# Expert weights in pieces of 8 KB: a change of the row order in the expert matmuls of a two-layer decoder trunk

## What is computed

```
for l in range(DEPTH):
    mod = silu(c) @ w_ada[l] + b_ada[l]                   # six rows of 1024: sh1, sc1, gt1, sh2, sc2, gt2
    u = x * (1 + sc1) + sh1
    mix = mlstm_and_conv(u @ w_in[l]) @ w_out[l]
    x = layer_norm(ALPHA * x + (1 + gt1) * mix)
    u = x * (1 + sc2) + sh2
    comb = route(u @ w_grp[l], u @ w_router[l])           # two experts a token, with weights
    for e in range(16):                                   # w_gate, w_up: (1024, 512); w_down: (512, 1024)
        h = silu(u @ w_gate[l][e]) * (u @ w_up[l][e])
        y = y + (h * comb[:, e]) @ w_down[l][e]
    x = layer_norm(ALPHA * x + (1 + gt2) * y)
```

## Time and profile before

| what | value |
|---|---|
| runs | 959.11, 959.91, 959.81 us (median 959.81) |
| span of the profiled execution | 958.0 us |
| TensorE busy (PE) | 851.8 us, 89% |
| weight loads into TensorE (PEld) | 437.7 us |
| VectorE, ScalarE busy | 246.4 us, 137.5 us |
| from HBM | 297.57 MB, 312 GB/s over the span |
| chain that ended last, by engine | PE 69%, SyncE's queue 14%, DMA 6%, VectorE 4%, ScalarE's queue 3% |

### The profile page before, as it was taken

One profiled execution on the slowest core, in us unless ns is written; L12 is line 12 of the kernel. 1 busy time (PEld: TensorE's weight loads), 2 busy tenths in 40 slices (PEclk: granted clock), 3 DMA queues, 4 the chain that ended last, 5 costly groups with the idle time before them and its releaser, 6 DMA issues.

```text
span 958.0 us, 9822 instructions
## 1 busy us (share of the span) xinstructions
PE 851.8 (89%) x3985; PEld 437.7 (46%) x3989; DVE 246.4 (26%) x679; ACT 137.5 (14%) x260; POOL 12.5 (1%) x42
## 2 busy tenths in 40 slices
PE   4349999998999999999879999999899999999881
PEld 1238478444534444344226847844443344434330
DVE  0012236236311110111063213614630111101106
ACT  1021110102201110011032111010310111101111
POOL 2100000000000000000001000000000000000000
PEclk9769999998999999999997999999999999999996
DMA  9993424768999999999999943486999999999981
GB/s 320 370 370 105 174 90 175 280 247 313 335 386 386 386 386 387 387 387 387 386 386 391 343 157 106 158 305 228 366 337 387 386 386 387 387 387 387 387 317 44
DMA packets 152562, 299.11 MB, mean 312 GB/s; under 512 B 8912, under 2 KB 9040, under 8 KB 152528
## 3 DMA queue, kind: packets, MB, share of 16 engines
q1 hardware_dynamic: 144288, 291.58, 83.2%
q0 software_dynamic: 1888, 6.82, 1.8%
q10 hardware_dynamic: 6352, 0.23, 0.5%
HBM read 297.57 MB, written 1.05 MB: 312 GB/s over the span
## 4 chain that ended last, share of the span: by engine, by line
PE 69%; SPq 14%; DMA 6%; DVE 4%; ACTq 3%; ACT 2%; issue 2%; another core or an unknown queue 0%; DVEq 0%
PE bank L474 16%; PE bank L441 15%; SPq L279 11%; PE bank L500 8%; PE bank L452 6%; PE bank L622 6%; PE bank L461 5%; DMA ring<-in_w_ada_dram 4%; PE bank L511 3%; PE bank L393 2%; DMA ring<-in_w_down_dram 2%; ACTq L755 2%; SPq L303 2%; DVE qT L951 2%; PE bank L562 1%
## 5 line engine op out<-in xcount | busy, mean ns | idle before, releaser
L474 PE MATMUL bank<-ring,qT 128*64 128x512 f32 x1024 | 227.1, 595 | 6.3 <-DMA ring<-in_w_gate_dram 3.4
L474 PEld LDWEIGHTS bank<-ring,qT 128*64 128x64 f32 x1024 | 73.4, 137 | 155.1 <-issue 144.9
L441 PE MATMUL bank<-uT,ring 128*128 128x256 f32 x640 | 139.9, 380 | 0.0
L441 PEld LDWEIGHTS bank<-uT,ring 128*128 128x128 f32 x640 | 121.1, 190 | 18.8 <-issue 2.7
L500 PE MATMUL bank<-ring,hb 128*64 128x512 f32 x512 | 113.8, 596 | 3.7 <-DMA ring<-in_w_down_dram 2.7
L959 DVE TENSOR_TENSOR o_sig<-o_sig,bank 128x512 f32<-128x512 f32 x16 | 11.0, 688 | 265.9 <-PE bank L474 241.5
L500 PEld LDWEIGHTS bank<-ring,hb 128*64 128x64 f32 x512 | 35.6, 137 | 70.7 <-issue 69.2
L461 PEld LDWEIGHTS bank<-ccT,X 128*128 128x128 f32 x512 | 58.5, 192 | 12.3 <-issue 11.4
L393 PE MATMUL bank<-ring,cond 128*32 128x512 f32 x384 | 50.4, 658 | 14.7 <-DMA ring<-in_w_ada_dram 13.4
L461 PE MATMUL bank<-ccT,X 128*128 128x128 f32 x512 | 61.2, 278 | 0.0
L511 PE MATMUL bank<-kT,hb 128*128 128x512 f32 x128 | 59.2, 605 | 0.0
(11 more groups left out here) (198 smaller groups left out, 495.2 us busy)
## 6 DMA issues: line engine op xcount, KB each, us to landing
ring<-in_w_gate_dram SPq DMA_DIRECT2D x32, 2048.0 KB, 19.2
ring<-in_w_up_dram SPq DMA_DIRECT2D x32, 2048.0 KB, 19.6
ring<-in_w_down_dram SPq DMA_DIRECT2D x32, 2048.0 KB, 18.1
ring<-in_w_ada_dram SPq DMA_DIRECT2D x24, 2048.0 KB, 14.1
ring<-in_w_in_dram SPq DMA_DIRECT2D x14, 2048.0 KB, 23.5
ring<-in_w_out_dram SPq DMA_DIRECT2D x4, 2048.0 KB, 8.0
gate_row<-in_b_ada_dram POOLq DMA_DIRECT2D x4, 512.0 KB, 9.6
ln_g<-in_ln_g_dram POOLq DMA_DIRECT2D x4, 512.0 KB, 11.2
```

Of the source, the lines that this page charges most:

```text
L441: last = pe.matmul(bank[4 + (b0 + q) % 4][:, 0:SEQ], w[:, kc, q * P:(q + 1) * P], uT[:, kc, :], start=(kc == 0), stop=(kc == KC - 1))
L474: last = pe.matmul(bank[bk][CAP * j:CAP * (j + 1), :], xg[:, 2 * k + h, CAP * j:CAP * (j + 1)], ring[s[h]][:, 4 * j + k, :], start=(h == 0 ...
```

## The change

An expert matrix is cut in two halves of the contraction rows, and in a half partition p now holds neighbouring rows: four for gate and up (rows 512 h + 4 p + j), two for down (rows 256 h + 2 p + j). For each expert, that is one piece of 8 KB that is contiguous in HBM and in SBUF, where there were four of 2 KB; a load is still 2 MB. The other operands follow the new order: `gather`, the transposes of X ahead of the router, and the columns of sh2 and sc2 take every fourth column (`rows_of`); the transposes of the hidden rows every second; the router's weights are loaded in the same order, in two loads each instead of one, and so are the biases of sh2 and sc2, with two more small loads on SyncE's queue and eight small transposes at the start. `down` runs through the rows of the first load for both halves of the output, then through those of the second, and signals three times instead of twice.

```diff
+        b_moe_rows = hb[0:4, :, :]
...
-        wg_all = w_gate.rearrange("l g e (k h p) f -> p (l g e k) h f", p=P, h=2)
-        wu_all = w_up.rearrange("l g e (k h p) f -> p (l g e k) h f", p=P, h=2)
-        wd_all = w_down.rearrange("l g e (k p) n -> p (l g e k) n", p=P)
+        wg_all = w_gate.rearrange("l g e (h p j) f -> p (l g e) h (j f)", p=P, j=4)
+        wu_all = w_up.rearrange("l g e (h p j) f -> p (l g e) h (j f)", p=P, j=4)
+        wd_all = w_down.rearrange("l g e (h p j) n -> p (l g e) h (j n)", p=P, j=2)
...
         def expert_released(eng, n, j):
 
-            eng.wait_ge((main.gate, main.up, main.down)[j // 2], 2 * n + j % 2 + 1)
+            if j < 4:
+                eng.wait_ge((main.gate, main.up)[j // 2], 2 * n + j % 2 + 1)
+            else:
+                eng.wait_ge(main.down, 3 * n + 2 * (j % 2) + 1)
 
         def expert_dma(eng, l, p, j, s, signal):
 
 
-            first = (l * EXPERTS + 2 * p) * 4
-            rows = slice(first, first + 8) if isinstance(first, int) else bass.ds(first, 8)
-            h = j % 2
-            src = (wg_all, wu_all)[j // 2][:, rows, h, :] if j < 4 else wd_all[:, rows, h * COLS:(h + 1) * COLS]
-            eng.dma_start(ring[s][:, :, :], src).then_inc(signal, 16)
+            first = l * EXPERTS + 2 * p
+            both = slice(first, first + 2) if isinstance(first, int) else bass.ds(first, 2)
+            src = (wg_all, wu_all, wd_all)[j // 2][:, both, j % 2, :]
+            dst = ring[s][:, :, :].rearrange("p (e r) n -> p e (r n)", e=2)
+            eng.dma_start(dst, src).then_inc(signal, 16)
+
+        def rows_of(c):
+
+            return slice(c // 4 * COLS + c % 4, (c // 4 + 1) * COLS, 4)
...
+                sp.dma_start(b_moe_rows[:, l, :], b_ada[l, 3 * D:5 * D].rearrange("(r n) -> r n", n=COLS)).then_inc(cols_landed, 16)
...
-                        last = pe.matmul(bank[6][:, 4 * i + q:4 * i + q + 1], part[:, i % 2, q * P:(q + 1) * P],
+                        cols = slice(q, COLS, 4) if i >= 4 else slice(q * P, (q + 1) * P)
+                        last = pe.matmul(bank[6][:, 4 * i + q:4 * i + q + 1], part[:, i % 2, cols],
                                          partials[:, 0:1], start=True, stop=True)
...
-            def transpose_x(ready, value, step):
+            def transpose_x(ready, value, step, cols):
...
-                        last = pe.transpose(bank[kc // 2][:, o:o + P], X[:, t, kc * P:(kc + 1) * P], ident[:, :])
+                        last = pe.transpose(bank[kc // 2][:, o:o + P], X[:, t, cols(kc)], ident[:, :])
...
-                                         X[:, t, kc * P:(kc + 1) * P], disp[b][:, t, :],
+                                         X[:, t, rows_of(kc)], disp[b][:, t, :],
...
-                            last = pe.matmul(bank[bk][CAP * j:CAP * (j + 1), :], xg[:, 2 * k + h, CAP * j:CAP * (j + 1)],
+                            last = pe.matmul(bank[bk][CAP * j:CAP * (j + 1), :], xg[:, 4 * h + k, CAP * j:CAP * (j + 1)],
...
-                    last = pe.transpose(bank[6][:, f * P:(f + 1) * P], hh[:, f * P:(f + 1) * P], ident[:, :])
+                    last = pe.transpose(bank[6][:, f * P:(f + 1) * P], hh[:, f // 2 * SEQ + f % 2:(f // 2 + 1) * SEQ:2],
+                                        ident[:, :])
...
 
             def down(S, n, s, here):
-                for half in range(2):
-                    if half == 0:
-                        pe.wait_ge(S.hTc, n + 1)
-                    else:
-                        pe.wait_ge(S.cTc, n + 1)
-                    here(half)
-                    for f in range(FC):
+
+                def part_of(h, half):
+                    for i in range(2):
+                        f = 2 * h + i
                         for j in range(2):
                             last = pe.matmul(bank[6 + half][CAP * j:CAP * (j + 1), :], hhT[:, f, CAP * j:CAP * (j + 1)],
-                                             ring[s[half]][:, 4 * j + f, :],
+                                             ring[s[h]][:, 4 * j + 2 * i + half, :],
                                              start=(f == 0), stop=(f == FC - 1), tile_position=(0, CAP * j))
-                    last.then_inc(S.down, 1)
+                    return last
+
+                pe.wait_ge(S.hTc, n + 1)
+                here(0)
+                part_of(0, 0)
+                pe.wait_ge(S.cTc, n + 1)
+                part_of(0, 1).then_inc(S.down, 1)
+                here(1)
+                part_of(1, 0).then_inc(S.down, 1)
+                part_of(1, 1).then_inc(S.down, 1)
...
+                for k in range(4):
+                    pe.transpose(bank[7][:, 192 + 16 * i + 4 * k:196 + 16 * i + 4 * k], b_moe_rows[:, i, k::4], ident[0:4, 0:4])
...
-                transpose_x(x_ready, 2 * T * l + 1, 1)
+                transpose_x(x_ready, 2 * T * l + 1, 1, rows_of)
...
-                act.wait_ge(S.down, 2 * n + 1)
+                act.wait_ge(S.down, 3 * n + 2)
...
-                        act.dma_start(w_route_sb[:, i, :, 0:G], w_grp[i].rearrange("(k p) n -> p k n", p=P)).then_inc(route_landed, 16)
-                        act.dma_start(w_route_sb[:, i, :, G:G + EXPERTS], w_router[i].rearrange("(k p) n -> p k n", p=P)).then_inc(route_landed, 16)
+                        for h in range(2):
+                            act.dma_start(w_route_sb[:, i, 4 * h:4 * h + 4, 0:G],
+                                          w_grp[i].rearrange("(h p j) n -> p h j n", p=P, j=4)[:, h, :, :]).then_inc(route_landed, 16)
+                            act.dma_start(w_route_sb[:, i, 4 * h:4 * h + 4, G:G + EXPERTS],
+                                          w_router[i].rearrange("(h p j) n -> p h j n", p=P, j=4)[:, h, :, :]).then_inc(route_landed, 16)
...
-                dve.wait_ge(S.down, 2 * n + 2)
+                dve.wait_ge(S.down, 3 * n + 3)
...
-                        dve.tensor_copy(b_ada_col[:, i, :], bank[7][:, 64 * i:64 * i + NMOD])
+                        dve.tensor_copy(b_ada_col[:, i, 0:3 * KC], bank[7][:, 64 * i:64 * i + 3 * KC])
+                        dve.tensor_copy(b_ada_col[:, i, 3 * KC:5 * KC].rearrange("p (r k) -> p r k", k=4),
+                                        bank[7][:, 192 + 16 * i:208 + 16 * i].rearrange("p (k r) -> p r k", k=4))
```

More of the change, by code:

```diff
@@ L314, in _ @@
                 with sp.If(more != 0):
-                    sp.wait_ge(main.down, 2 * PAIRS * (l + 1))
+                    sp.wait_ge(main.down, 3 * PAIRS * (l + 1))
                     with sp.Fori(0, ROUNDS - 1) as r:
@@ L318, in _ @@
                             for j in range(6):
-                                sp.wait_ge(over[l].down, 2 * (r * PAIRS + p))
+                                sp.wait_ge(over[l].down, 3 * (r * PAIRS + p))
                                 expert_dma(sp, l, p, j, slot(l, MOE + j), over_landed[l][j])
-                    sp.wait_ge(over[l].down, 2 * (ROUNDS - 1) * PAIRS)
+                    sp.wait_ge(over[l].down, 3 * (ROUNDS - 1) * PAIRS)
             for t in range(T):
@@ L553, in _ @@
                 if l == 0:
-                    transpose_x(x_landed, 16 * T, 0)
+                    transpose_x(x_landed, 16 * T, 0, lambda kc: slice(kc * P, (kc + 1) * P))
                 else:
-                    transpose_x(x_ready, 2 * T * l - T + 1, 1)
+                    transpose_x(x_ready, 2 * T * l - T + 1, 1, lambda kc: slice(kc * P, (kc + 1) * P))
                 pe.wait_ge(uT_act, 8 * l + 4)
@@ L1096, in _ @@
                 dve.wait_ge(logT_done, l + 1)
-                dve.wait_ge(route_landed, 16 * 4 * DEPTH)
+                dve.wait_ge(route_landed, 16 * 6 * DEPTH)
                 dve.tensor_scalar(logT[:, :], bank[6][0:G + EXPERTS, 0:SEQ], b_route_col[:, l:l + 1], None,
```

4 lines of the change are left out of this document (2 added, 2 removed).

## The result

The changed kernel takes **1022.82 us** (median of 4 runs, 1022.6 to 1023.41); the kernel before, on the same chip, 959.86 us (4 runs, 959.11 to 963.9). The ratio is 1.0638, with a 95% interval from 1.0613 to 1.0662: slower. The forecast was 1011 us with a range to 1018; the sign is right, the size lies 4.8 us above the range. The profiled execution has a span of 1020.1 us and its own time is 1022.62 us.

A forecast was written before the change was run, and what follows sets the result against it. TensorE's pace was taken as the bound, with load waits only at layers' ends and between layers. 958.0 - 13.7 + 56.8 + 6.9 + 0.7 + 1.0 = 1009.7 us span, plus 1.8 gives 1011.5 us; range 944 to 1018 us.

The forecast's parts named there:

- the step costs: Likeliest case: weight loads reading X with a step of four get slower; 990 to 1018 us, chance 0.62.
- The waits gone: TensorE's waits for loads at both layers' ends and between the layers vanish with faster 8 KB transfers: -13.7 us.
- The gather: Step of four doubles the gather's weight load column price: 229 instead of 118 ns a record, +56.8 us.
- The rival with VectorE's surcharge of 85 ns: Gather's step costs less, 85 ns a load, partly hidden under the matmul: 998 us; chance included in 0.62.
- The other readers: Transposes of X and extraction records of units 4, 5 and 9, read with a step of four: +6.9 us.
- The start: Two small SyncE loads ahead of w_ada, +0.7 us, and four more loads on ScalarE's queue, +1.0 us.
- The hidden rows with a step of two: Four transposes of the hidden rows, priced at nothing; 7 us more if they doubled as well.
- The combine copy's earlier wait: Down's earlier wait for the combine copy costs nothing under four matmuls; without that cover up to 1.8 us a pair.
- 8 KB packets at 432 GB/s: Expert loads: rate estimated from 2 KB and 4 KB packets; a 2 MB load takes 4.9 instead of 5.4 us.
- The rival of a free step: A step of four is free in the gather's weight loads, only the waits change: 947.8 us, chance 0.30.
- VectorE's row: A VectorE reduction of 32 floats takes 207 ns with a step of four, 185 in a row; nearest evidence for weight loads.
- The rival of ScalarE's queue: Small loads at the start decide: merged pieces save up to 24 us, a cost by load adds up to 27; chance 0.05.

The follow-up runs named there:

- Experiment 3: The kernel before with the 8 KB loads alone, all operands in the old order: 946.44 us, ratio 0.9838.
- experiment 2: The kernel before with only the gather reading every fourth column of X, loads still in 2 KB pieces: 1009.71 us, ratio 1.0491.
- experiment 8: The kernel before with each router load split in two, rows in the old order: 965.2 us, ratio 1.0017.
- experiment 5: The kernel before with only the gather reading every second column of X: 962.25 us, ratio 1.0016.
- 6: The kernel before with only the gather reading every eighth column of X: 1015.08 us in a single run.
- 11: The changed kernel with the gather reading ScalarE's reordered copy of X, late router loads and contiguous extraction of units 4, 5, 8, 9: 924.62 us, ratio 0.9576.
- 12: The kernel before with ScalarE's router and layer 1 gate loads issued after the first modulation: 935.12 us, ratio 0.9693.
- experiment 1: The changed kernel with the gather reading blocks of 128 neighbouring columns of X again: 960.7 us, ratio 0.9999.

## Why the prediction came out as it did

The likeliest case was the right one: "the step costs", at the gather, through weight loads that nothing hides. What was missed is its size: the sum's term for the gather was 5.3 us too small, those for the other readers and for the start 2.1 and 3.6 us, and the range of that case, 990 to 1018 us, took in too little above. By its own steps:

- **The waits gone**, -13.7 us: measured -14.3. Experiment 3, with the pieces alone, gains 13 to 15 us. But the cause given, the faster transfer, is only half of it: in the changed kernel slower gathers alone would have ended them (experiment 2). The prediction added the two terms and got the right sum, since the waits go once either way; that much is luck.
- **The gather**, +56.8 us: measured +62.1. This is the largest of the three misses; alone it would have left the forecast, at 1016.8 us, inside its range. I took 0.86 ns for a column of a weight load, from the difference of a 64-column and a 128-column load, and doubled 128 of them: 107 ns more a record. What doubled was the whole interval of a load that stands alone, 122 ns: 245 ns, as the extraction now shows, and 240 in the gather. Doubling 122 instead of adding 107 would have given 126 ns x 512 = 64.5 us. The row was in hand, the fixed part was wrongly kept out of it. The rival with VectorE's surcharge of 85 ns (998 us) is out by more.
- **The other readers**, +6.9: measured +9.0. The readers themselves cost 7.9: units 4 and 5 1.95 us a layer where 1.7 was put, unit 9 and the transposes of X 1.9 and 2.1 us where 1.8 was put. The other 1.1 us are stretches in which the granted clock differed: 1.9 us more where the router's matmuls of layer 1 ran at half the clock after the change and not before it (L652, 5.51 against 3.63 us), and 0.7 us less in two others (the router's of layer 0, the gates' of layer 1). What set the clock there isn't known.
- **The start**, +1.7: measured +5.3. SyncE's two small loads cost the 0.8 to 1.0 us that were put on them. The split router loads cost about 3 us (experiment 8), where 1.0 was taken for four more end markers, a price that stood on no row; the markers are there, 64 packets more, but what makes the split cost 3 us isn't known. The rest is the clock. From 8 to 35 us the changed kernel's trace shows a granted clock of 0.79 instead of 0.94, and the fourth unit's matmuls take 3.64 instead of 1.92 us; later in the stage one group of projections (L462) took 14.00 us, 1.7 less than before. Experiment 2, whose start is that of the kernel before, shows the same 3.64 us and, for the same projections, the same 14.00 us, and that stage ends 2.4 us later there. So one to two of the 5.3 us are the difference between two executions and not the change.
- **The hidden rows with a step of two** at nothing: right, four records take 0.63 us as before, and experiment 5 shows a step of two at 6 ns a record in the gather.
- **The combine copy's earlier wait, the later bank of the down output, the eight small transposes** at nothing: right, a pair grew by the gather's 3.90 us and nothing else.
- **8 KB packets at 432 GB/s**: whole packets, at 417 to 423 GB/s, so the estimate from 2 KB and 4 KB rows was 2 to 4% too high; it didn't matter.
- **The rival of a free step** (947.8 us, 0.30) would by its own sum have been right in sign had the price been under 21 ns a record; it is 122. Experiment 5 (6 ns) lies on the free side of that number, 2 and 6 (122 and 127 ns) on the other. No row of the kernel before told which side a step of four is on, so that the 0.62 for the dear side was a bet on VectorE's row, and it came out.
- **The rival of ScalarE's queue**: the pieces were not merged (6416 packets), and the split cost 3 us, not 27.
- **What would show it wrong** named ScalarE's first modulation moving by more than 3 us: it moved by 5.7.

The Trainium skill, "SBUF — State Buffer", section "Door 1: The DMA port swizzle", was weighed as two rules. The lines of 16 bytes with two hits wanted agree with the runs at both sides: 124 ns for a step of two, 240 for four, 245 for eight, here in weight loads of TensorE; a step of three, which would test the line itself, was not run. The same note's remark that 4 fp32 can be strided for free, read as a step of four, does not: by it experiment 2 would have taken 961 us, and it took 1009.7.

The misses add up to +5.3 (gather), +2.1 (readers), +3.6 (start), -0.6 (waits): 10.4 us. The span forecast was 1009.7 us and the one measured 1020.1, the same 10.4 more. The median time is 11.3 us above the 1011.5 forecast, since it lies 2.7 us above the span after the change and not 1.8. All three sizes fell on the same side, and the range of 7 us above the forecast had room for the hidden rows only, whose step turned out free.

## What to carry to other kernels

A row order that suits the DMA engines is a permutation that somebody has to undo: let an engine that idles undo it once (ScalarE, 3.9 us a layer), not, with a step of four floats or more, the stationary operand of a matmul that is read eight times a layer and already goes at the pace of its weight loads. A row order with a step of two, and so pieces of 4 KB, was not run as a whole; by the gather's 6 ns a record (experiment 5) its order would cost an estimated 3 us. Two figures of one kernel tell whether a weight load is hidden: the interval of its records, and the same load's interval where the matmul is one column wide; where they agree, each nanosecond on the load is paid in full. And before a faster transfer is bought, ask what else ends the same waits, and read the queue ahead of the first computation: moving eight lines of small loads was worth 26 us, the 8 KB pieces 10.5 (numbers 11 and 12) to 15 (experiment 3).

## What the runs showed of the hardware

- A float32 weight load of 128 columns by the step between columns: 1, 2, 4 and 8 floats give records of 118, 124, 240 and 245 ns and loads of 192, 197, 329 and 335 ns in the gather.
- The length of one load is not its price. The hidden rows' loads went from 141 to 207 ns in experiment 1 with a step of two, and their four records still take 0.63 us; in experiment 2 they read 167 ns at step one. In these traces the time follows the interval of the records; why these loads read longer and the gather's with a step of two do not stays open.
- DMA rates by the size of a packet: 387 GB/s at 2 KB, 416 at 4 KB (a stretch of 2 us only), 417 to 423 at 8 KB. By that one stretch, most of what larger pieces give is there at 4 KB.
- ScalarE copies 1024 floats a partition, read with a step of four and written contiguously, in 1.97 us.
- Splitting four small loads with pieces of 16 and 64 bytes in two, bytes unchanged, kept ScalarE's queue about 3 us longer (32.4 against 29.1 in experiment 8, 32.0 in the changed kernel).
- The granted clock of one stretch differs between executions of the same instructions: 8 to 35 us show 0.94 in the kernel before and 0.75 in experiment 2, whose start is the same.
